# First output projection: products ordered by high and low weights, transposed tiles ahead of weights, last two tiles normalised one by one

## The chip, the core and the metric

The kernel runs on one core of a Trainium2 chip. The metric is the device time of one execution in microseconds (us), here the median of three runs. The five instruction queues of the core are PE (TensorE, with PEld for its loads of the stationary operand), DVE (VectorE), ACT (ScalarE), POOL (GpSimd) and SP (SyncE, which issues the transfers here). Each takes its instructions in the order in which the program wrote them, and they wait for each other through semaphores.

## The reference, cut to what matters

The program computes three blocks one after the other on 1024 tokens of width 1024. The stage in question is the end of the first block and the layer norm that opens the second:

```python
y = jnp.concatenate([y_conv, y_ret], axis=-1) @ w_out[l]     # (1024, 2048) @ (2048, 1024)
h = h + gate * y
return _rmsnorm(h, final_g)
...
x = layer_norm(x, ln_in_g, ln_in_b)                          # second block, LN_EPS = 1e-5
proj = x @ w_in + b_in                                       # what follows the stage
```

## The kernel before

**Splitting.** Every float32 matrix product is made of three products of reduced parts. A tile is split into a high part (ScalarE copies it to the type fp32r) and a low part (VectorE subtracts the high part from the original), and PE adds up hi*hi, hi*lo and lo*hi in the same PSUM bank (`products`, L370 to L372). The low*low product is left out in both kernels.

**Tiling.** The projection contracts 2048 channels in NK = 16 steps of 128 (`K_ORDER`: the eight tiles of the retention half `yr`, then the eight of the convolution half `yc`). Its eight token tiles of 128 go in three groups, `O_GROUPS` = (0,1,2), (3,4,5), (6,7), because each token tile of a group needs a pair of PSUM banks (2 x 512 columns) for the whole group: `bank_of` = pair 0, pair 3, pair 2. A step of group 0 or 1 is 3 tokens x 2 halves x 3 products = 18 matmuls of 128x128 on 128x512, a step of group 2 is 12. In all 16 x 18 + 16 x 18 + 16 x 12 = 768.

**Weights.** Each step needs one tile of `w_out` (128x1024): SP loads it into `wo_raw` (two buffers, L1306, after the low part two tiles before it is made), ACT makes `wo_hi` (L1422, after PE has finished the step two before, semaphore `wo_used`), DVE makes `wo_lo` (L1293, after `wo_hi`). In group 0 the same loops also split the input tile into `yr_hi`/`yc_hi` (L1424) and `yr_lo`/`yc_lo` (L1298). The last two tiles of a group serve the first two steps of the next, so 44 tiles are loaded for 48 steps. PE waits at the head of a step for `wo_lo` (semaphore `o1_wlo`).

**End of a group.** When a token tile's sums are complete (`o1_mm`), DVE multiplies them by the gate into `tmp` (L1474, which frees the bank pair: `gate_ok`, in the rows below `o1_gate`), and adds the residual tile `xo` (L1476). ACT squares and takes the root (L1450, L1455), DVE scales and takes the statistics (L1479 to L1485), ACT takes the second root (L1460), DVE centres and finishes (L1489, L1494), and `h_ok` (in the rows `o1_h`) is raised. SP stores the tile as `h`. In the next group, ahead of its steps 10, 11 and 12, PE transposes the three tiles (L1358), ACT makes `h_hi` of the transposed tile (L1431) and DVE `h_lo` (L1500). `highs(upto)` and `out_lows(upto)` are the places in the queues of ACT and DVE at which the parts of the next weights are made.

**Behind the last group** PE computes the first half (512 tokens) of the channels 0, 1 and 2 of the next projection (`channel`, 24 matmuls each), transposes tiles 6 and 7, and computes the second halves, channel 0 by the loop at L1400 to L1404. The channel weights are split by ACT (`ch_hi`, L1648) and POOL (`ch_lo`, L1690). ACT's `ch_hi` of channel 0 stands behind the last `h_hi` of group 1's tiles and waits until tile 5 is stored (`h2_out[2]`), since it reuses that buffer.

## Time and profile before

| | |
|---|---|
| median of 3 runs | 2764.65 us (2763.58 to 2766.03) |
| span of the profiled execution | 2763.9 us |
| PE busy | 2689.4 us, 97% |
| DVE busy | 2086.6 us, 75% |
| ACT busy | 1069.2 us, 39% |
| POOL busy | 477.0 us, 17% |
| share of the chain that ended last | PE 80%, DVE 14%, issue 2%, ACT 1%, DMA 1% |

The profile is of one execution, and the trace gives its span from the first to the last instruction. The page counts how long each engine was busy. The timeline lists the instructions of an engine by their start, with the idle time before one in brackets and what released it. A matmul's printed duration (0.39 us) is longer than the distance to the next one, since matmuls overlap; distances are taken between starts. The chain of waits follows the end of the program back from releaser to releaser.

### The profile page before, as it was taken

The page shows a single profiled execution, that of the slowest core. Times are in us where ns is not written, and L with a number is a line of the kernel's source. Part 1 is how long each engine was busy: PE and PEld are TensorE (multiplying, and loading weights), DVE is VectorE, ACT ScalarE, POOL GpSimd, SP SyncE. Part 2 cuts the span into 40 slices and gives each one's busy share as a digit, 9 for nine tenths or more (in the row PEclk, how much of TensorE's full clock was granted, in tenths as well). Part 3 has the DMA queues.
Part 4 walks back from the last instruction along what each step waited for, and adds up shares of the span by engine and source line. Part 5 has one row for each costly group of instructions (what it writes and reads, how often), then busy time and mean ns, then how long its engine had stood idle before and what let it go on. Part 6 is the DMA issues. An engine that isn't in the chain of part 4 may idle for free.

```text
span 2763.9 us, 33573 instructions
## 1 busy us (share of the span) xinstructions
PE 2689.4 (97%) x13192; PEld 2199.6 (80%) x13192; DVE 2086.6 (75%) x2796; ACT 1069.2 (39%) x1599; POOL 477.0 (17%) x254
## 2 busy tenths in 40 slices
PE   6999999999999999999999999999999999999998
PEld 5888888888888878778875678888887888888887
DVE  6999998873724663369998886688186988887978
ACT  5111112243413332245537751365232554555332
POOL 0000000000100002001210001354211656655000
PEclk8999999999999999999999999999999999999999
DMA  5312222224325452011101032100132222225431
GB/s 223 116 63 69 94 97 61 84 92 142 99 107 175 136 176 90 31 62 39 47 30 36 32 123 96 46 31 23 62 115 80 96 77 89 87 77 188 170 99 61
DMA packets 97710, 250.18 MB, mean 91 GB/s; under 512 B 7361, under 2 KB 34369, under 8 KB 96018
## 3 DMA queue, kind: packets, MB, share of 16 engines
q1 hardware_dynamic: 93010, 231.49, 24.4%
q10 hardware_dynamic: 4288, 15.73, 1.5%
q8 instruction: 105, 1.72, 0.2%
q0 software_dynamic: 256, 0.82, 0.1%
q14 instruction: 51, 0.42, 0.1%
HBM read 202.92 MB, written 45.09 MB: 90 GB/s over the span
## 4 chain that ended last, share of the span: by engine, by line
PE 80%; DVE 14%; issue 2%; ACT 1%; DMA 1%; DVEq 0%; ACTq 0%
PE pair L370 16%; PE pair L372 16%; PE pair L371 16%; PE pair L3657 7%; PE pair L3242 5%; PE pair L3244 5%; PE pair L3245 5%; DVE counted L1942 3%; PE pair L2593 2%; DVE reached L1993 1%; PE pair L2156 1%; DVE top_i L1999 1%; PE pair L1754 1%; PE pair L2172 1%; PE pair L2185 1%
## 5 line engine op out<-in xcount | busy, mean ns | idle before, releaser
L370 PE MATMUL pair<-u_hi,w_hi 128*128 128x512 f32 x768 | 302.1, 393 | 1.2 <-PEq L92 0.9
L641 DVE SCALAR_TENSOR_TENSOR conv_acc<-aT,cols,conv_acc 128x1024 f32<-128x1024 f32 x232 | 297.9, 1284 | 6.7
L371 PE MATMUL pair<-u_lo,w_hi 128*128 128x512 f32 x768 | 300.3, 391 | 0.0
L372 PE MATMUL pair<-u_hi,w_lo 128*128 128x512 f32 x768 | 300.3, 391 | 0.0
L370 PEld LDWEIGHTS pair<-u_hi,w_hi 128*128 128x128 f32 x768 | 145.2, 189 | 32.7 <-issue 2.4
L371 PEld LDWEIGHTS pair<-u_lo,w_hi 128*128 128x128 f32 x768 | 145.0, 189 | 30.6 <-issue 0.7
L372 PEld LDWEIGHTS pair<-u_hi,w_lo 128*128 128x128 f32 x768 | 145.0, 189 | 30.6
L370 PE MATMUL pair<-h_hi,ch_hi 128*128 128x512 f32 x392 | 153.8, 392 | 2.8 <-ACT ch L1824 2.6
L372 PE MATMUL pair<-h_hi,ch_lo 128*128 128x512 f32 x392 | 152.7, 389 | 0.0
L371 PE MATMUL pair<-h_lo,ch_hi 128*128 128x512 f32 x392 | 152.6, 389 | 0.0
L1014 POOL TENSOR_TENSOR yrT<-yrT,gate_c 128x1024 f32<-128x1024 f32 x8 | 18.9, 2366 | 758.1 <-ACT yrT L907 758.1
L3192 POOL TENSOR_TENSOR op_lo<-w_sum,op_hi 128x512 fp32r<-128x512 f32 x80 | 137.6, 1721 | 33.6 <-ACT op_hi L3322 33.6
L454 DVE TENSOR_TENSOR w_lo<-wt,w_hi 128x1024 fp32r<-128x1024 f32 (+1 forms) x64 | 69.8, 1091 | 77.0 <-ACT w_hi L450 76.9
L3242 PE MATMUL pair<-t_hi,op_hi 128*128 128x512 f32 x320 | 124.6, 389 | 0.0
L3245 PE MATMUL pair<-t_hi,op_lo 128*128 128x512 f32 x320 | 124.5, 389 | 0.0
L3244 PE MATMUL pair<-t_lo,op_hi 128*128 128x512 f32 x320 | 124.5, 389 | 0.0
L1690 POOL TENSOR_TENSOR ch_lo<-wt,ch_hi 128x1024 fp32r<-128x1024 f32 x17 | 40.7, 2395 | 464.7 <-ACT ch_hi L1648 464.7
L450 ACT ACTIVATE w_hi<-wt 128x1024 fp32r<-128x1024 f32 (+1 forms) x64 | 60.8, 950 | 142.8 <-PE pair L372 135.3
L1293 DVE TENSOR_TENSOR wo_lo<-wo_raw,wo_hi 128x1024 fp32r<-128x1024 f32 x44 | 54.0, 1228 | 66.5 <-ACT wo_hi L1422 66.4
L370 PE MATMUL pair<-h_hi,p_hi 128*128 128x512 f32 x256 | 103.6, 405 | 0.0
L372 PE MATMUL pair<-h_hi,p_lo 128*128 128x512 f32 x256 | 100.2, 392 | 0.0
L371 PE MATMUL pair<-h_lo,p_hi 128*128 128x512 f32 x256 | 99.7, 389 | 0.0
(510 smaller groups left out, 7105.1 us busy)
## 6 DMA issues: line engine op xcount, KB each, us to landing
wt<-in_w_ch SPq DMA_DIRECT2D x60, 512.0 KB, 3.4
wo_raw<-in_w_out SPq DMA_DIRECT2D x44, 512.0 KB, 3.6
wt<-in_w_up SPq DMA_DIRECT2D x10, 1024.0 KB, 4.9
w_raw<-in_w_up SPq DMA_DIRECT2D x10, 1024.0 KB, 4.8
g_spill<-g_stage SPq DMA_DIRECT2D x40, 256.0 KB, 2.2
ada_mod<-in_ada_mod SPq DMA_DIRECT2D x4, 2048.0 KB, 14.3
wt<-in_w_conv SPq DMA_DIRECT2D x16, 512.0 KB, 3.5
qk<-qk_st SPq DMA_DIRECT2D x8, 1024.0 KB, 6.4
```

The source lines that it names most:

```text
L370: nc.tensor.matmul(bank, w[0], x[0], start=(first and k == 0), stop=False)
L371: nc.tensor.matmul(bank, w[0], x[1], start=False, stop=False)
L372: return nc.tensor.matmul(bank, w[1], x[0], start=False, stop=(last and k == n_k - 1))
L450: nc.scalar.activation(slot_view(w_parts[0], n), slot_view(wt, n), ACT.Copy).then_inc(job_hi, 1)
L454: nc.vector.tensor_tensor(slot_view(w_parts[1], n), slot_view(wt, n), slot_view(w_parts[0], n).bitcast(F32), ALU.subtract).then_inc(job_lo, 1)
L641: nc.vector.scalar_tensor_tensor(dst, x, w, conv_acc[:], ALU.mult, ALU.add).then_inc(conv_step, 1)
L1942: nc.vector.tensor_scalar(to, scores(t), least, None, op, ALU.add, accum_out=found[:, t - 2:t - 1]).then_inc(counts_ok, 1)
L3192: nc.gpsimd.tensor_tensor(op_lo[j], operand(w, j), op_hi[j].bitcast(F32), ALU.subtract).then_inc(op_lo_ok, 1)
L3242: nc.tensor.matmul(bank, hi[:, k, :], x_hi[:, k, :], start=(j in opens and k == 0), stop=False, skip_group_check=True)
L3244: nc.tensor.matmul(bank, hi[:, k, :], x_lo[:, k, :], start=False, stop=False, skip_group_check=True)
L3245: last = nc.tensor.matmul(bank, lo[:, k, :], x_hi[:, k, :], start=False, stop=(k == 3), skip_group_check=True)
L3657: last = nc.tensor.matmul(dn_bank(p, t), x[:, i, t * P:(t + 1) * P], w[:, i, :], start=(p in (P1, P7, P2) and c == kind == i == 0), stop=( ...
```

## The change

It edits only this stage. On PE a step no longer runs through `products` token by token: all tokens' hi*hi come first, then all x_lo*w_hi, then all x_hi*w_lo, and the waits for `x_hi`, `x_lo`, `wo_hi` and `wo_lo` stand each ahead of the products that use the part. On ACT and DVE `h_hi` and `h_lo` of a transposed tile come one weight tile earlier in the queue (`at0 + 11 + j` for `at0 + 12 + j`). For the last group, roots and reciprocals are made for each tile by itself, tile 6 is finished before tile 7 is centred, and the transposes of tiles 6 and 7 stand inside the first half of channel 2.

```diff
--- before.py
+++ after.py
@@ -1365,35 +1365,46 @@
                 k = K_ORDER[s % NK]
                 if g and i in (10, 11, 12):
                     transposes(3 * (g - 1) + i - 10)
-                pe.wait_ge(wo_lo_ok, s + 1)
+                pe.wait_ge(wo_hi_ok, s + 1)
                 if g == 0:
-                    pe.wait_ge(x_lo_ok, i + 1)
-                for j, t in enumerate(O_GROUPS[g]):
-                    if g and i == 0:
-                        pe.wait_ge(gate_ok, 3 * (g - 1) + j + 1)
-                    if n == 0 and j == 0:
-                        pe.wait_ge(ot_ok, KT * TT)
-                    if n == 0 and j == 1:
-                        pe.wait_ge(pw_out, KT - 1)
-                    for h in range(2):
-                        last = products(bank_of[j][:, h, :],
-                                        [x[:, k % KT, t * P:(t + 1) * P] for x in x_parts(k)],
-                                        [w[:, s % 2, h * HALF:(h + 1) * HALF] for w in wo_parts], i, NK)
-                    if i == NK - 1:
-                        last.then_inc(o1_mm, 1)
+                    pe.wait_ge(x_hi_ok, i + 1)
+                x_hi, x_lo = x_parts(k)
+                w_hi, w_lo = (w[:, s % 2, :] for w in wo_parts)
+                for x, w in ((x_hi, w_hi), (x_lo, w_hi), (x_hi, w_lo)):
+                    if x is x_lo and g == 0:
+                        pe.wait_ge(x_lo_ok, i + 1)
+                    if w is w_lo:
+                        pe.wait_ge(wo_lo_ok, s + 1)
+                    for j, t in enumerate(O_GROUPS[g]):
+                        if x is x_hi and w is w_hi:
+                            if g and i == 0:
+                                pe.wait_ge(gate_ok, 3 * (g - 1) + j + 1)
+                            if n == 0 and j == 0:
+                                pe.wait_ge(ot_ok, KT * TT)
+                            if n == 0 and j == 1:
+                                pe.wait_ge(pw_out, KT - 1)
+                        for h in range(2):
+                            last = nc.tensor.matmul(bank_of[j][:, h, :], x[:, k % KT, t * P:(t + 1) * P],
+                                                    w[:, h * HALF:(h + 1) * HALF],
+                                                    start=(i == 0 and x is x_hi and w is w_hi),
+                                                    stop=(i == NK - 1 and w is w_lo))
+                        if i == NK - 1 and w is w_lo:
+                            last.then_inc(o1_mm, 1)
                 if i == NK - 1:
                     pe.wait_ge(o1_mm, O_GROUPS[g][-1] + 1)
                     pe.sem_inc(wo_used, 1)
                 else:
                     last.then_inc(wo_used, 1)
-            for n in range(3):
-                if n == 1:
-                    pe.wait_ge(gate_ok, 7)
-                if n == 2:
-                    pe.wait_ge(gate_ok, 8)
-                channel(pe, n, 0)
-            for t in O_GROUPS[-1]:
-                transposes(t)
+            channel(pe, 0, 0)
+            pe.wait_ge(gate_ok, 7)
+            channel(pe, 1, 0)
+            pe.wait_ge(gate_ok, 8)
+            for k in range(KT):
+                if k == KT - 3:
+                    transposes(TT - 2)
+                if k == KT - 2:
+                    transposes(TT - 1)
+                channel_step(pe, 2, k)
             pe.wait_ge(tr_ok, TT)
             bank, w_hi, w_lo = pair[CH_PAIR[0]][:, 1, :], ch_hi_of(0), ch_part_lo[0]
             for k in range(KT):
@@ -1449,17 +1460,25 @@
                         act.wait_ge(sq_done, t)
                     nc.scalar.activation(junk1[:], xo[j][:], ACT.Square,
                                          accum_out=ssq[:, j:j + 1]).then_inc(sq_done, 1)
+                    if g == 2:
+                        act.wait_ge(sq_done, t + 1)
+                        nc.scalar.activation(sd1[:, j:j + 1], ssq[:, j:j + 1], ACT.Sqrt, bias=eps6[:],
+                                             scale=1.0 / D).then_inc(rms_ok, 1)
                     if j == 1:
                         highs(at0 + 3)
-                act.wait_ge(sq_done, tokens[-1] + 1)
-                nc.scalar.activation(sd1, ssq, ACT.Sqrt, bias=eps6[:], scale=1.0 / D).then_inc(rms_ok, 1)
-                highs(at0 + 6)
                 if g == 2:
                     channel_high(act, 2)
-                act.wait_ge(bnv_ok, tokens[-1] + 1)
-                nc.scalar.activation(sd2, mv1[:, :, 1], ACT.Sqrt, bias=eps5[:]).then_inc(sd_ok, 1)
+                    for j, t in enumerate(tokens):
+                        act.wait_ge(bnv_ok, t + 1)
+                        nc.scalar.activation(sd2[:, j:j + 1], mv1[:, j, 1:2], ACT.Sqrt, bias=eps5[:]).then_inc(sd_ok, 1)
+                else:
+                    act.wait_ge(sq_done, tokens[-1] + 1)
+                    nc.scalar.activation(sd1, ssq, ACT.Sqrt, bias=eps6[:], scale=1.0 / D).then_inc(rms_ok, 1)
+                    highs(at0 + 6)
+                    act.wait_ge(bnv_ok, tokens[-1] + 1)
+                    nc.scalar.activation(sd2, mv1[:, :, 1], ACT.Sqrt, bias=eps5[:]).then_inc(sd_ok, 1)
                 for j, t in enumerate(tokens):
-                    highs(at0 + 12 + j)
+                    highs(at0 + 11 + j)
                     evacuate(t)
                 if g == 1:
                     act.wait_ge(h2_out[2], 32)
@@ -1516,7 +1535,7 @@
                 at0 = NEW * (g + 1)
                 if g:
                     for j, t in enumerate(O_GROUPS[g - 1]):
-                        out_lows(dve, NEW * g + 12 + j)
+                        out_lows(dve, NEW * g + 11 + j)
                         low_part(t)
                 out_lows(dve, at0 + 2)
                 add(0, tokens[0])
@@ -1524,6 +1543,19 @@
                 for j, t in enumerate(tokens[1:]):
                     add(j + 1, t)
                 out_lows(dve, at0 + 3)
+                if g == 2:
+                    for j, t in enumerate(tokens):
+                        dve.wait_ge(rms_ok, 3 + j)
+                        nc.vector.reciprocal(rr1[:, j:j + 1], sd1[:, j:j + 1]).then_inc(rr_ok, 1)
+                        dve.wait_ge(rr_ok, 3 + j)
+                        normalize(j, t)
+                    for j, t in enumerate(tokens):
+                        center(j, t)
+                        dve.wait_ge(sd_ok, 3 + j)
+                        nc.vector.reciprocal(rv1[:, j:j + 1], sd2[:, j:j + 1]).then_inc(rv_ok, 1)
+                        dve.wait_ge(rv_ok, 3 + j)
+                        finish(j, t)
+                    continue
                 dve.wait_ge(rms_ok, g + 1)
                 nc.vector.reciprocal(rr1, sd1).then_inc(rr_ok, 1)
                 dve.wait_ge(rr_ok, g + 1)
```

PE, group 0 to group 1. Before, the next group's first step takes token 0 with six matmuls and then waits for token 1's pair (`pair<-` names the matmul's output, behind it the moving and the stationary operand):

```order
L371 MATMUL pair<-wo_lo,yc_hi 128x512
L372 MATMUL pair<-wo_hi,yc_lo 128x512
L370 MATMUL pair<-wo_hi,yc_hi 128x512 [waits o1_mm,o1_gate,o1_wlo]
L371 MATMUL pair<-wo_lo,yc_hi 128x512
L372 MATMUL pair<-wo_hi,yc_lo 128x512
L370 MATMUL pair<-wo_hi,yc_hi 128x512
L371 MATMUL pair<-wo_lo,yc_hi 128x512
L372 MATMUL pair<-wo_hi,yc_lo 128x512
L370 MATMUL pair<-wo_hi,yc_hi 128x512 [waits o1_gate]
```

PE, the same place after; the first two rows are the end of group 0's last step:

```order
L1387 MATMUL pair<-wo_lo,yc_hi 128x512 [waits o1_wlo]
L1387 MATMUL pair<-wo_lo,yc_hi 128x512 x5
L1387 MATMUL pair<-wo_hi,yc_hi 128x512 [waits o1_mm,o1_gate,o1_whi]
L1387 MATMUL pair<-wo_hi,yc_hi 128x512
L1387 MATMUL pair<-wo_hi,yc_hi 128x512 [waits o1_gate]
L1387 MATMUL pair<-wo_hi,yc_hi 128x512
L1387 MATMUL pair<-wo_hi,yc_hi 128x512 [waits o1_gate]
L1387 MATMUL pair<-wo_hi,yc_hi 128x512
L1387 MATMUL pair<-wo_hi,yc_lo 128x512 x6
L1387 MATMUL pair<-wo_lo,yc_hi 128x512 [waits o1_wlo]
L1387 MATMUL pair<-wo_lo,yc_hi 128x512 x5
```

The waits for the three bank pairs now stand two matmuls apart instead of six, and the low parts' products stand last.

ACT, the end of group 1's tiles, before:

```order
L1422 ACTIVATE wo_hi<-wo_raw 128x1024 [waits o1_used,wo_in0]
L1431 ACTIVATE h_hi<-pair 128x8x128 [waits o1_tr]
L1422 ACTIVATE wo_hi<-wo_raw 128x1024 [waits o1_used,wo_in1]
L1431 ACTIVATE h_hi<-pair 128x8x128 [waits o1_tr]
L1648 ACTIVATE ch_hi_677<-wt 128x1024 [waits ch_w0,h2_out2]
L1422 ACTIVATE wo_hi<-wo_raw 128x1024 [waits o1_used,wo_in0]
L1422 ACTIVATE wo_hi<-wo_raw 128x1024 [waits o1_used,wo_in1]
L1648 ACTIVATE ch_hi_678<-wt 128x1024 [waits ch_w1,o1_mm]
```

and after:

```order
L1433 ACTIVATE wo_hi<-wo_raw 128x1024 [waits o1_used,wo_in0]
L1442 ACTIVATE h_hi<-pair 128x8x128 [waits o1_tr]
L1680 ACTIVATE ch_hi_677<-wt 128x1024 [waits ch_w0,h2_out2]
L1433 ACTIVATE wo_hi<-wo_raw 128x1024 [waits o1_used,wo_in1]
L1433 ACTIVATE wo_hi<-wo_raw 128x1024 [waits o1_used,wo_in0]
L1433 ACTIVATE wo_hi<-wo_raw 128x1024 [waits o1_used,wo_in1]
L1680 ACTIVATE ch_hi_678<-wt 128x1024 [waits ch_w1,o1_mm]
```

Three weight tiles' high parts, those of steps 41 to 43 of the 44 loaded (counted from 0), stand behind `ch_hi_677` and its wait for the store `h2_out2`, where two did before.

PE, the last two tiles, after:

```order
L1358 MATMUL pair<-ident,xo_611 128x128 [waits h2_lo_ok,o1_h]
L1358 MATMUL pair<-ident,xo_611 128x128 x7
L370 MATMUL pair<-h_hi,ch_hi_679 128x512
L371 MATMUL pair<-h_lo,ch_hi_679 128x512
L372 MATMUL pair<-h_hi,ch_lo_676 128x512
L1358 MATMUL pair<-ident,xo_612 128x128 [waits o1_h]
L1358 MATMUL pair<-ident,xo_612 128x128 x7
```

Before, both sets of transposes stood behind the whole of channel 2's first half; now nine of its matmuls follow the first set, three of them ahead of the second.

## Rows read from the trace of the kernel before

**Rows 1.** The page: span, and granted clock in 40 slices.
```profile
span 2763.9 us, 33573 instructions
...
PEclk8999999999999999999999999999999999999999
```

**Rows 2.** Windows by stretch; busy us and count of each engine, then clock.
```profile
914.00:983.00 69.00, 68.15 (x312) 56.05 (x311) 43.09 (x43) 21.50 (x25) 0.00 (x0) 1.00 0.51 152
983.00:1042.00 59.00, 52.17 (x229) 39.69 (x227) 44.48 (x45) 22.37 (x26) 2.41 (x1) 1.00 0.50 152
1042.00:1067.00 25.00, 23.64 (x111) 19.43 (x111) 21.14 (x31) 9.73 (x12) 5.18 (x2) 1.00 0.41 144
```

**Rows 3.** Chain that ended last, 980 to 1043: by line; start, us, what.
```profile
by line: DMA wo_raw<-in_w_out 23.7%; DVE wo_lo L1293 17.2%; DVE small L1483 6.2%; DVE xo L1479 5.9%; DVE xo L1476 5.9%; DVE tmp L1474 5.9%; PE pair L370 5.5%; ACT wo_hi L1422 5.1%; PE pair L372 5.1%; PE pair L371 5.1%; DVE xo L1494 3.9%; DV
...
1013.87 3.62 DMA wo_raw<-in_w_out
1019.86 6.00 DMA wo_raw<-in_w_out
```

**Rows 4.** Waits of PE, 836 to 1095: total us, times, longest.
```profile
PE pair L370 <- DVE wo_lo L1293: 4.8, 7, 1.5
PE pair L1358 <- DVE h_lo L1500: 1.6, 2, 1.2
```

**Rows 5.** Timeline of PE: start, us, instruction [idle before <-releaser].
```profile
867.17 0.47 PE L370 MATMUL pair<-wo_hi,yr_hi 128*128 128x512 f32 x1 [0.74 <-DVE yr_lo L1298]
...
913.51 0.39 PE L370 MATMUL pair<-wo_hi,yc_hi 128*128 128x512 f32 x1
...
916.00 0.39 PE L372 MATMUL pair<-wo_hi,yc_lo 128*128 128x512 f32 x1
916.70 0.47 PE L370 MATMUL pair<-wo_hi,yc_hi 128*128 128x512 f32 x1 [0.30 <-PE pair L372]
...
920.23 0.50 PE L370 MATMUL pair<-wo_hi,yc_hi 128*128 128x512 f32 x1 [0.55 <-DVE tmp L1474]
```

**Rows 6.** Timeline of DVE: yr_lo, two multiplies, and the slow add.
```profile
865.80 1.22 DVE L1298 TENSOR_TENSOR yr_lo<-yrT,yr_hi 128x1024 fp32r<-128x1024 f32 x1
...
913.71 1.23 DVE L1474 TENSOR_TENSOR tmp<-pair,gate_bc 128x1024 f32<-128x1024 f32 x1 [1.93 <-PE pair L372]
...
918.95 1.23 DVE L1474 TENSOR_TENSOR tmp<-pair,gate_bc 128x1024 f32<-128x1024 f32 x1
...
1044.57 2.11 DVE L1476 TENSOR_TENSOR xo<-xo,tmp 128x1024 f32<-128x1024 f32 x1
```

**Rows 7.** Timeline of ACT at the end of group 2.
```profile
1029.74 1.06 ACT L1422 ACTIVATE wo_hi<-wo_raw 128x1024 fp32r<-128x1024 f32 x1 [1.88 <-DMA wo_raw<-in_w_out]
...
1031.61 1.05 ACT L1648 ACTIVATE ch_hi<-wt 128x1024 fp32r<-128x1024 f32 x1
```

**Rows 8.** Timeline of SP's queue; landing of stores, 1010 to 1062.
```profile
1024.35 0.43 SPq L1313 DMA_DIRECT2D h<-xo  x1
...
DMA to landing us min/median/max: 2.6/5.2/6.9
```

**Rows 9.** Timeline of PE at the last two tiles.
```profile
1058.58 2.16 PE L1358 MATMUL pair<-ident,xo 128*128 128x128 f32 x16
...
1061.91 0.50 PE L1400 MATMUL pair<-h_hi,ch_hi 128*128 128x512 f32 x1 [1.17 <-ACT h_hi L1435]
1062.25 0.40 PE L1401 MATMUL pair<-h_hi,ch_lo 128*128 128x512 f32 x1
...
1065.71 0.62 PE L1404 MATMUL pair<-h_lo,ch_hi 128*128 128x512 f32 x2
```

**Rows 10.** Timeline of DVE and POOL at the last two tiles.
```profile
1040.69 1.23 DVE L1474 TENSOR_TENSOR tmp<-pair,gate_bc 128x1024 f32<-128x1024 f32 x1 [2.26 <-PE pair L372]
...
1048.23 0.18 DVE L1528 RECIPROCAL small<-small 128x3 f32<-128x3 f32 x1 [1.55 <-ACT small L1455]
...
1043.19 2.41 POOL L1690 TENSOR_TENSOR ch_lo<-wt,ch_hi 128x1024 fp32r<-128x1024 f32 x1 [8.05 <-ACT ch_hi L1648]
```

## The prediction

> **What bounds the kernel now.** I read the page first. Its span and its clock row [rows 1] say that TensorE (PE) is busy nearly always at the full granted clock, so what can be won is the little that PE stands idle in the edited stage, and what can be lost is any new idle time there. The stage is the first output projection, from about 850 to 1067 us of the span. The windows by stretch [rows 2] give the size of the prize. In group 1 (914 to 983) PE is idle 0.85 of 69 us, in group 2 (983 to 1042) 6.83 of 59, in the tail (1042 to 1067) 1.36 of 25. With 0.74 at 867 the stage holds some 10 us of idle PE, 0.4% of the time. Then I asked what sets the length of each stretch. Group 1 is PE's own: 18 matmuls a step, one every 0.2265 us (from 913.51 to 916.00 there are 11 [rows 5]), 4.08 us a step. Group 2 is not: the chain that ended last [rows 3] holds PE for only 16% there; its largest parts are the weight transfers (23.7%), VectorE's low parts (17.2%) and VectorE's adds and normalisation. After the stage, PE or the work released by it is the chain, without any earlier start that could absorb a shift, so I carry a shift of the stage's end to the end one for one.
>
> The profiled execution has a span of 2763.9 us; the median of the three runs is 2764.65, 0.75 above it. I work out a difference against the trace and add it to the median. This kernel's measurement can tell about 0.2% (5.5 us) from no change, so faster means under 2759.1, slower over 2770.2.
>
> **Part 1, PE starts a step with the high parts.** Once in group 0 and seven times in group 2, PE stands before a step's first matmul until VectorE's low parts are there [rows 4, 5]. In group 0 this is the step at 867.17 [rows 5]: it waited for yr_lo, made from 865.80 to 867.02 [rows 6]; its high parts had been ready at 865.6. The last matmul before it began at 866.04, so in the new order the step begins at 866.27 and wants yr_lo for its matmuls 7 to 12, at 867.6. The hole goes: 867.17 - 866.27 and 0.1 of refill, **-1.0**. The rest of group 0 is PE's own pace, so it is kept.
>
> **Part 2, what the same reordering does to the end of a group.** This is the cost, and it follows from the order. Before, a step finishes token 0's bank pair after 6 of its 18 matmuls, token 1's after 12, token 2's after 18, and the next group begins with six matmuls on token 0. After, all hi*hi come first, then lo*hi, then hi*lo, so the three bank pairs of the last step finish after 14, 16 and 18 matmuls, and in the next group's first step PE wants token 1's pair after two matmuls and token 2's after four (the waits for o1_gate in the order above). VectorE frees each pair with one multiply, and its queue has multiply, add, multiply, add, multiply: the multiplies start at 913.71, 916.33 and 918.95, 2.62 us apart [rows 6] (the second has no row there), so the pairs come free 1.23 us after each.
> First place, group 0 to group 1: the first multiply can start 8 matmuls later, 8 x 0.2265 = 1.81 us, so 915.52; pairs free at 916.75, 919.37, 921.99. PE, at the old times, starts on token 0 at 916.8 (before 916.70), on token 1 at 919.4 and on token 2 at 922.0, and has 14 matmuls left, 14 x 0.2265 + 0.1 refill = 3.3: the step ends at 925.3. Before, token 2 began at 920.23 with 6 matmuls left: 920.23 + 1.36 + 0.1 = 921.7 [rows 5]. **+3.6**. Nothing hides it: ScalarE's next high part waits for that step's end, and group 1 is at PE's pace throughout.
> The Trainium skill (Perfetto Trace Analysis, section Matmuls) says that independent groups of matmuls should rotate through PSUM banks so that the evacuation of one overlaps the next one's matmuls. It speaks against this change. Read strictly, with nothing left to overlap, the multiply would start only with the 18th matmul, 4 x 0.2265 = 0.9 later, and this term would be 4.5; the issue order still leaves that 0.9, so the sum keeps 3.6.
> Second place, group 1 to group 2: two tokens only. PE's first step would end 2.3 us later (pair 1 free at 987.56 + 1.23 = 988.8, 10 matmuls left, 991.2, against 988.9). But here PE is not what counts. From 983.1, the group's first multiply, to 1013.9 the chain runs through VectorE's queue, where the low parts lie between adds and normalisations; from there on the weight loop sets the pace (low part, transfer of 3.6 to 6.0, high part 1.07, low part 1.23) [rows 3]. All of it starts with the first multiply, so it moves by **+1.8**. Against this stands the only place where part 1 pays in group 2: PE needs the low part for a step's last 4 matmuls of 12, not the first, so a step ends 4 matmuls after its low part and no longer 12: 8 x 0.2265 = **-1.8**. The two cancel. The sum of the waits that the trace shows in group 2 is so no gain: it is the slack of an engine that waits for a supply whose length the change doesn't shorten.
>
> **Part 3, transposes served ahead of weights.** Twice in group 2 (1.6 us in all [rows 4]) PE waits for h_lo of the previous tile before it transposes the next, because VectorE's h_lo stands behind a low part whose weights have not landed. With the new order these two waits go, but PE then only reaches the next weights sooner. Worked through with the trace's durations (times below include the +1.8): transposes at 1020.6, 1024.3 and 1027.9, step 40 ends at 1031.5 instead of 1033.0, and step 41 finds no high part: its weights land at 1031.5, since their transfer is released by low part 39. Gain nil. In the new order of ScalarE's queue, moreover, the high part of step 41 has gone behind ch_hi, which waits until the last of the first six tiles is stored. Before, the queue had high part 41 at 1029.74, h_hi, then ch_hi at 1031.61 without a wait [rows 7]. The store is issued behind the weights' transfer, at 1024.35, and stores here land in 5.2 us (median) to 6.9 (longest) [rows 8]; with 1.8 added, 1031.4 to 1033.1. High part 41 then starts at 1032.4 to 1034.1 instead of 1031.5, and so do low part 41, transfer 43, high part 43 and the last step. It would end at 1042.3 to 1043.9, against 1041.85: +0.5 to +2.1, I take **+1.3**, the middle, since the transfers around it are at the long end (6.0 and 5.3 us). If the store is early, it is 0. In group 1 the same move costs nothing: a step of 4.08 us covers h_hi and h_lo, and the next high part is needed only at its end.
>
> **Part 4, the last two tiles one by one.** Before: PE has finished channel step 2 at about 1058.5, transposes at 1058.58 and 1059.81, and goes on at 1061.91 [rows 9]. After, the transposes stand before the sixth and seventh k of that channel, 15 matmuls in, at 1056.5 at the earliest. VectorE decides. Its first multiply comes 4 matmuls later, 1040.69 + 0.91 = 1041.60. Two multiplies and adds take 5.99 us with the slow add of 2.11 beside POOL [rows 6, 10]: 1047.6. ScalarE's root for tile 6 is long done, so the idle 1.55 us before 1048.23 goes. Then reciprocal 0.21, normalisation 2.77, reciprocal 0.21, normalisation 3.35 with its slow instruction, centre 1.22, reciprocal 0.21, finish 1.22: tile 6 ready at 1056.8; centre, reciprocal, finish 2.7 more: tile 7 at 1059.5, against 1059.6 before. If the two slow instructions (0.88 and 0.58 over the ordinary 1.23 and 1.28) miss POOL, they are 1055.3 and 1058.0. From the second transposes to L1400 it took 2.10 us [rows 9]; with 6 matmuls behind the transposes 2.25. PE goes on between 1060.5 and 1061.9: -1.5 to 0. I take **-0.8**. The extra small instructions (ScalarE two roots more of 0.30, VectorE two reciprocals more of 0.2) are in these sums. The third channel's low part is wanted at 1053.1 and was made by 1052.0; it comes at most 0.9 later.
> The Trainium skill (GPSIMD Engine Reference, section Key points) says that GpSimd shares its SBUF interfaces with VectorE and contends with instructions with two SBUF inputs. The rows agree: the add of xo and tmp took 2.11 us beside ch_lo, the multiply out of PSUM 1.23. By that rule both adds would now meet ch_lo, this term would be about 0, and the sum 0.8 higher; the rows at hand show one slow add at a time, so the middle stands.
>
> **Sum.** -1.0 + 3.6 + (1.8 - 1.8) + 1.3 - 0.8 = **+3.1 us**: 2764.65 + 3.1 = **2767.7**. Bounds: low -1.0 + 3.4 - 0.5 + 0 - 1.5 = +0.4, high -0.9 + 3.8 + 0.5 + 2.1 - 0 = +5.5 (0.2 on the gate for latencies, 0.5 on the cancelling pair), so the likeliest case has 2765.0 to 2770.2.
>
> **Rivals.**
> A, the low parts really were the brake. If VectorE and the transfers can run ahead in group 2 once PE no longer waits for the low part, all 6.8 us of idle time there [rows 2] go and only PE's own stall of 2.3 comes: -1.0 + 3.6 - 6.8 + 2.3 - 0.8 = -2.7, 2762.0. For it: the waits view names wo_lo as the longest. Against: the chain [rows 3]. If the gate stall at the first place were missing too, it would be -6.3, 2758.3, faster; against that stands VectorE's strict sequence of 2.62 us.
> B, slower: matmuls come less densely. The new order changes the bank with every matmul where the old one did so every third, and the stationary tile every second. The old rows show no gap at a change of bank. But where L1400 and L1401 alternate, 15 matmuls take 3.46 us, 0.2307 each, from 1062.25 to 1065.71 [rows 9]. The stage has 768 matmuls: 768 x (0.2307 - 0.2265) = 3.2 us more, 2770.9. It decides from 0.230 on: then 2.5 us more carry the time over 2770.2.
>
> **How the numbers follow.** The forecast 66%, A 14% (about half of it below 2759.1, with the stall missing or other gains), B 20%, with what of a worse tail goes beyond 2.1. The range: cutting a tenth at either side gives 2761.5 to 2772.0. Faster 0.08, same 0.72, slower 0.20: of the forecast hardly anything lies over 2770.2, of B nearly all.
>
> **What would show it.** Right: in the first step of group 1 two stops of about 2.2 us each before L1387, released by the multiply into tmp; no wait at 867; the first step of group 1 some 3.6 us longer; in group 2 PE's waits now mostly for wo_hi, with the stretch as long as before or 1 to 2 us longer; ch_hi waiting for a store ahead of high part 41; the pause around the last transposes smaller by about 1 us. Wrong: group 2 shorter by several us (A), or matmuls spaced over 0.230 us inside a step (B).

## The result, and the profile after

The changed kernel takes **2774.95 us** (median of 6 runs, 2773.9 to 2776.56), the kernel before 2764.69 (6 runs). The ratio is 1.0038, with a 95% interval of 1.0026 to 1.0049. The forecast was 2767.7 with a range up to 2772.0: the direction of the sum was right, its size was not, and the time is outside the range. The kernel became slower by more than the 0.2% that can be told.

To see where, I cut the edited stage at five matmuls that both traces have (start times in the timelines of TensorE): the first matmul of the first output projection, the first of group 1, of group 2, of the channel work, and the first of channel 0's second half (L1400 before, L1411 after).

| stretch, us | before | after | difference | forecast |
|---|---|---|---|---|
| group 0 | 66.78 | 65.97 | -0.81 | -1.0 |
| group 1 | 69.42 | 74.76 | +5.34 | +3.6 |
| group 2 | 56.04 | 58.63 | +2.59 | +1.3 |
| tail | 19.75 | 20.36 | +0.61 | -0.8 |
| together | 211.99 | 219.72 | +7.73 | +3.1 |

Outside these stretches the span grew by another 1.4 us (0.46 ahead of the stage, 0.92 behind it). Nothing there is edited, and the traces of all twelve kernels put the start of the stage anywhere from 848.6 to 850.4 and the rest behind it at 1701.5 to 1704.0, so I don't count it as the change's.

The page has a longer span and the same clock row as before [rows 1]:

```profile
span 2773.1 us, 33578 instructions
...
PEclk8999999999999999999999999999999999999999
```

Finer windows tell what those 40 digits can't. They answer to [rows 2] (columns: TensorE busy and count, weight loads, VectorE, ScalarE, GpSimd, granted clock, DMA share, GB/s):

```profile
914.00:918.00 4.00, 2.55 (x11) 1.49 (x9) 2.85 (x3) 0.50 (x1) 0.00 (x0) 1.00 0.00 0
918.00:922.00 4.00, 1.72 (x3) 1.00 (x4) 3.80 (x4) 1.80 (x4) 0.00 (x0) 0.54 0.00 0
922.00:926.00 4.00, 4.00 (x12) 3.09 (x11) 0.70 (x1) 0.00 (x0) 0.00 (x0) 0.61 0.00 0
926.00:930.00 4.00, 4.00 (x19) 3.27 (x19) 1.96 (x3) 2.40 (x4) 0.00 (x0) 1.00 0.00 0
930.00:985.00 55.00, 55.00 (x256) 45.77 (x255) 34.06 (x35) 16.80 (x17) 0.00 (x0) 1.00 0.57 182
985.00:992.00 7.00, 6.30 (x27) 4.62 (x25) 2.23 (x2) 0.00 (x0) 0.00 (x0) 1.00 0.25 75
992.00:998.00 6.00, 4.37 (x13) 3.48 (x14) 5.12 (x5) 2.52 (x5) 0.00 (x0) 0.72 0.02 4
```

From 918 to 926 TensorE is granted 0.54 and 0.61 of its clock, so for most of the time the lower of its two levels, 1.2 GHz. Windows cut still finer put the whole fall between 918.3 and 925.2:

```profile
917.10:918.30 1.20, 0.00 (x0) 0.00 (x0) 1.07 (x2) 0.80 (x1) 0.00 (x0) 1.00 0.00 0
918.40:925.10 6.70, 4.82 (x11) 3.34 (x12) 4.10 (x4) 1.40 (x4) 0.00 (x0) 0.50 0.00 0
```

The window from 922 to 926 is fully busy and holds 12 matmuls instead of 19. The same happens at 992 to 998, at the edge of groups 1 and 2. The rest of group 1 (930 to 985) is without a hole and at full clock. TensorE's timeline at the first edge, beside [rows 5] (start, us, instruction, idle before and its releaser):

```profile
914.33 1.52 PE L1387 MATMUL pair<-wo_lo,yc_hi 128*128 128x512 f32 x6
916.35 0.70 PE L1387 MATMUL pair<-wo_hi,yc_hi 128*128 128x512 f32 x2 [0.50 <-DVE tmp L1493]
918.88 1.22 PE L1387 MATMUL pair<-wo_hi,yc_hi 128*128 128x512 f32 x2 [1.82 <-DVE tmp L1493]
921.50 1.22 PE L1387 MATMUL pair<-wo_hi,yc_hi 128*128 128x512 f32 x2 [1.40 <-DVE tmp L1493]
922.52 2.76 PE L1387 MATMUL pair<-wo_hi,yc_lo 128*128 128x512 f32 x6
925.08 1.59 PE L1387 MATMUL pair<-wo_lo,yc_hi 128*128 128x512 f32 x6
926.51 1.54 PE L1387 MATMUL pair<-wo_hi,yc_hi 128*128 128x512 f32 x6
927.89 1.52 PE L1387 MATMUL pair<-wo_hi,yc_lo 128*128 128x512 f32 x6
```

The two stops that the forecast named are here, 1.82 and 1.40 us, each ended by VectorE's multiply. What it did not have is the row at 922.52: six matmuls in 2.56 us (to 925.08), where six take 1.36 at 927.89 (to 929.25). The 14 matmuls from 921.50 to 926.51 needed 5.0 us instead of 3.3. The clock was already low at 918.4, inside the first stop (917.06 to 918.88) and ahead of the second.

Group 2 loses its first time in a place that the forecast had called unimportant. VectorE's timeline after, and the same low part (tile 30) before:

```profile
989.73 1.22 DVE L1493 TENSOR_TENSOR tmp<-pair,gate_bc 128x1024 f32<-128x1024 f32 x1 [4.88 <-PE pair L1387]
...
998.87 1.23 DVE L1293 TENSOR_TENSOR wo_lo<-wo_raw,wo_hi 128x1024 fp32r<-128x1024 f32 x1 [1.42 <-ACT wo_hi L1433]
```

```profile
990.77 1.22 DVE L1293 TENSOR_TENSOR wo_lo<-wo_raw,wo_hi 128x1024 fp32r<-128x1024 f32 x1
```

Counted from group 2's first matmul (986.12 before, 991.11 after), this low part starts at 4.65 before and at 7.76 after. ScalarE's high part ahead of it is the reason, since it may overwrite its buffer only when TensorE has ended the slowed first step. Then, at the end of the group, comes the store wait that the forecast did have, beside [rows 7]:

```profile
997.78 1.06 ACT L1433 ACTIVATE wo_hi<-wo_raw 128x1024 fp32r<-128x1024 f32 x1 [1.76 <-PE pair L1387]
...
1037.47 1.06 ACT L1680 ACTIVATE ch_hi<-wt 128x1024 fp32r<-128x1024 f32 x1 [1.50 <-DMA h<-xo]
1038.43 1.04 ACT L1433 ACTIVATE wo_hi<-wo_raw 128x1024 fp32r<-128x1024 f32 x1
```

The store wait had company that the forecast did not have. Behind channel 0's high part GpSimd makes its low part, and in the new queue order that falls on VectorE's low part of tile 41, which takes 2.56 us where the low part of tile 30 above took 1.23. (Before, it met the low part of tile 42, which took 1.60.) It ends 1.08 us behind GpSimd; what that means is worked out under e8.

```profile
1038.60 2.38 POOL L1722 TENSOR_TENSOR ch_lo<-wt,ch_hi 128x1024 fp32r<-128x1024 f32 x1 [260.67 <-ACT ch_hi L1680]
...
1039.50 2.56 DVE L1293 TENSOR_TENSOR wo_lo<-wo_raw,wo_hi 128x1024 fp32r<-128x1024 f32 x1 [2.27 <-ACT wo_hi L1433]
```

The chain that ended last, by line, from 990 to 1043, answers to [rows 3]: TensorE's products now hold 29.0% of it and the weight transfers 12.4%, against 16% and 23.7%.

```profile
by line: PE pair L1387 29.0%; DVE wo_lo L1293 15.5%; DMA wo_raw<-in_w_out 12.4%; DVE small L1502 7.3%; DVE xo L1498 7.0%; issue 6.2%; PE pair L1358 4.9%; DVE tmp L1493 4.7%; DVE xo L1508 4.6%; ACT wo_hi L1433 4.1%; DVE xo L1513 2.4%; DVE xo
```

In the tail the idle 1.55 us of [rows 10] is gone, but tile 7's normalisation takes 2.99 us beside GpSimd's low part, where tile 6's takes 1.28; the transposes wait for it twice:

```profile
1055.12 1.28 DVE L1498 SCALAR_TENSOR_TENSOR xo<-xo,small,fg_bc 128x1024 f32<-128x1024 f32 x1
...
1058.04 2.99 DVE L1498 SCALAR_TENSOR_TENSOR xo<-xo,small,fg_bc 128x1024 f32<-128x1024 f32 x1
...
1057.56 2.39 POOL L1722 TENSOR_TENSOR ch_lo<-ch_raw,ch_hi 128x1024 fp32r<-128x1024 f32 x1 [3.63 <-ACT ch_hi L1680]
...
1065.19 1.09 PE L1358 MATMUL pair<-ident,xo 128*128 128x128 f32 x8 [0.92 <-DVE xo L1513]
...
1067.78 1.09 PE L1358 MATMUL pair<-ident,xo 128*128 128x128 f32 x8 [0.80 <-DVE xo L1513]
```

### The profile page after: what moved, and what is told of

Read it like the earlier page. It is cut to its first block, busy times and chain, and to the rows that moved or that the text cites. A ratio compares the mean times of both kernels' runs of the same rounds, so it can differ in the third digit from the quotient of the medians.

```text
span 2773.1 us, 33578 instructions
## 1 busy us (share of the span) xinstructions
PE 2694.8 (97%) x13192; PEld 2202.8 (79%) x13192; DVE 2083.1 (75%) x2798; ACT 1070.4 (39%) x1601; POOL 479.5 (17%) x254
## 4 chain that ended last, share of the span: by engine, by line
PE 83%; DVE 11%; issue 2%; ACT 1%; DMA 0%; DVEq 0%; ACTq 0%
PE pair L370 15%; PE pair L372 15%; PE pair L371 15%; PE pair L3689 7%; PE pair L1387 5%; PE pair L3276 5%; PE pair L3274 5%; PE pair L3277 5%; DVE counted L1974 2%; PE pair L2625 2%; DVE reached L2025 1%; PE pair L2188 1%; PE pair L1786 1%; PE pair L2204 1%; PE pair L2217 1%
```

## The experiments

Two questions stood: what of the loss is the edge between groups, and why the clock falls; and what of the loss at the end of group 2 and in the tail is the order of ScalarE's queue. All edits are to the changed kernel, unless said otherwise. The stage lengths of all, in us (cut as above), beside the ratio to the kernel before on the same chip:

| kernel | group 0 | group 1 | group 2 | tail | together | ratio [95%] |
|---|---|---|---|---|---|---|
| before | 66.78 | 69.42 | 56.04 | 19.75 | 211.99 | |
| after | 65.97 | 74.76 | 58.63 | 20.36 | 219.72 | 1.0038 [1.0026, 1.0049] |
| e1 | 65.77 | 69.41 | 59.68 | 19.60 | 214.46 | 1.0007 [0.9998, 1.0015] |
| e2 | 65.97 | 71.21 | 58.54 | 20.36 | 216.08 | one run |
| e3 | 65.97 | 73.01 | 59.10 | 20.36 | 218.44 | 1.0030 [1.0018, 1.0043] |
| e4 | 65.97 | 74.77 | 59.25 | 20.49 | 220.48 | 1.0029 [1.0017, 1.0041] |
| e5 | 65.97 | 74.50 | 57.50 | 20.36 | 218.33 | 1.0023 [1.0014, 1.0033] |
| e6 | 65.77 | 69.40 | 54.34 | 20.35 | 209.86 | 0.9992 [0.9983, 1.0001] |
| e7 | 65.77 | 69.40 | 53.23 | 20.36 | 208.76 | 0.9991 [0.9982, 0.9999] |
| e8 | 65.97 | 75.31 | 59.49 | 20.49 | 221.26 | 1.0031 [1.0019, 1.0043] |
| e9 | 65.77 | 69.40 | 54.10 | 19.45 | 208.72 | 0.9987 [0.9978, 0.9996] |
| e10 | 65.97 | 74.70 | 60.30 | 19.46 | 220.43 | 1.0029 [1.0018, 1.0041] |

Groups 0 and 1 and the tail repeat within some 0.3 us wherever their code is the same; e8's group 1, 0.55 over that of after, is the exception. Group 2 doesn't: e10 has exactly the code of after there and took 1.67 us more. Of this, 1.50 is there when ScalarE starts channel 0's high part (47.86 us behind the group's first matmul, 46.36 in after), which had waited 2.75 us for the store instead of 1.50. So much of the scatter is that store wait, which is part of the change's own cost and differs from run to run. A single trace can tell differences of 2 us or more in group 2; smaller ones are indications.

**e1, products token by token in each group's last step and in the first step of groups 1 and 2.**

```diff
+                if (g and i == 0) or i == NK - 1:
+                    pe.wait_ge(wo_lo_ok, s + 1)
...
+                    for j, t in enumerate(O_GROUPS[g]):
...
+                            last = products(bank_of[j][:, h, :],
...
+                else:
                     for x, w in ((x_hi, w_hi), (x_lo, w_hi), (x_hi, w_lo)):
```

> The changed kernel, but in the last step of each group and in the first step of the next the products run token by token again, as before the change; all other steps start with the high parts. Theory S (the loss is made at the group edges: the three bank pairs come free late, PE stops twice, and its granted clock falls to half): no stops in the first step of group 1 beyond the old 0.3 and 0.55 us, clock 1.00 there; group 1 begins its second step near 921.0 and not 926.5; group 2 still gets its low parts at VectorE's pace, but starts its adds 1.8 us earlier than the changed kernel and ends each step 4 matmuls after the low part, so the first channel matmul comes near 1041 to 1042 and not at 1049.7. Total 2766 to 2768 us, of which 1.3 to 2.5 are the ch_hi behind the store and the tail. Rival R (the reordering costs everywhere, by a wider spacing of matmuls or by later release of the weights): still over 2771 us, with the surplus spread over all steps.

Measured: 2767.64 us. Group 1 is back at 69.41, the whole 5.35 us. So the entire loss of group 1 is made in the steps at the edges, and the new order costs nothing in the 14 others. Group 2 gained nothing, at 59.68. Channel 0's high part waited 2.15 us for the store, and TensorE stood for 2.52 us ahead of the step of tile 41. Then the group's own last step, now wanting its low part first, waited 1.94 us and ran at the lower clock:

```profile
1030.40 1.20 PE L1401 MATMUL pair<-wo_hi,yc_hi 128*128 128x512 f32 x4 [2.52 <-ACT wo_hi L1447]
...
1038.86 0.50 PE L370 MATMUL pair<-wo_hi,yc_hi 128*128 128x512 f32 x1 [1.94 <-DVE wo_lo L1293]
1039.17 0.62 PE L371 MATMUL pair<-wo_lo,yc_hi 128*128 128x512 f32 x1
1039.59 0.63 PE L372 MATMUL pair<-wo_hi,yc_lo 128*128 128x512 f32 x1
```

The last two start 0.42 us apart, not 0.2265. Behind the longer pause of 2.52 us the clock stayed at 1.00 (windows from 1028 to 1038.8). The expectation had the first channel matmul at 1041 to 1042; it came at 1043.59.

**e2, only the first steps of groups 1 and 2 token by token.** The edit is that of e1 with the condition `g and i == 0`.

> The changed kernel, but only the first step of groups 1 and 2 runs token by token; in the last step of each group the bank pairs are still finished after 14, 16 and 18 matmuls. VectorE's multiplies then start 1.8 us later than in e1, 2.62 us apart, and PE reaches token 1 after six matmuls and token 2 after twelve. Theory S: token 1's pair is free 2.6 us after PE's start on token 0, 1.4 needed, so a stop of about 1.2 us, then another of 1.2; the first step of group 1 ends near 923.5 in the changed kernel's times (926.5), about 2.5 us after e1. Whether the clock falls for stops of 1.2 us is open: if it doesn't, the clock belongs to the length of the stops and not to their number. Rival R: no difference to e1.

Measured: 2769.58 us in its one run, group 1 at 71.21, 1.79 over before. The stops at the edge are shorter, with six matmuls between them instead of two:

```profile
918.72 0.50 PE L370 MATMUL pair<-wo_hi,yc_hi 128*128 128x512 f32 x1 [0.90 <-DVE tmp L1507]
...
921.33 0.50 PE L370 MATMUL pair<-wo_hi,yc_hi 128*128 128x512 f32 x1 [0.96 <-DVE tmp L1507]
921.67 0.39 PE L371 MATMUL pair<-wo_lo,yc_hi 128*128 128x512 f32 x1
```

From the second one behind each stop on the matmuls are 0.23 us apart: no fall of the clock. What is left, 1.79, is near the 8 x 0.2265 = 1.81 by which the last step in the new order frees its first bank pair later. The stops were shorter than the 1.2 us expected.

**e3, the stops filled.** Ahead of the waits for the second and third pair, TensorE first waits for the idle pair `pair[1]` to be free and does 8 matmuls into it, whose result nobody reads. It does the same work as the changed kernel otherwise, and those 16 or 8 matmuls more at each edge.

```diff
                             if g and i == 0:
+                                if j:
+                                    pe.wait_ge(pw_out, KT)
+                                    if g == 2:
+                                        pe.wait_ge(h2_lo_ok, 3)
+                                    for _ in range(8):
+                                        nc.tensor.matmul(pair[1][:, 0, :], x[:, k % KT, t * P:(t + 1) * P],
+                                                         w[:, 0:HALF], start=True, stop=True)
                                 pe.wait_ge(gate_ok, 3 * (g - 1) + j + 1)
```

> The changed kernel, with eight idle matmuls (into a free bank, results unused) ahead of each wait for a further bank pair in the first steps of groups 1 and 2, which last 1.8 us and lie inside the stops of 1.8 and 1.4 us plus a margin. The waits for VectorE stay as they are. Theory S with the clock as a part of its own: PE never pauses for over 0.5 us, the granted clock stays at 1.00, the first step of group 1 ends 1.7 us earlier (near 924.8), and group 2 gets its first high part about 1 us earlier; total 2 to 3 us below the changed kernel, 2772 to 2773. If the clock has no part in it, the total is the same as the changed kernel's or more, 2775 and above.

Measured: 2774.0 us, group 1 at 73.01. The same windows as above, in e3:

```profile
918.00:922.00 4.00, 3.97 (x17) 2.74 (x16) 3.80 (x4) 1.19 (x3) 0.00 (x0) 1.00 0.00 0
922.00:926.00 4.00, 4.00 (x20) 3.30 (x19) 0.56 (x2) 1.57 (x2) 0.00 (x0) 1.00 0.00 0
...
992.00:998.00 6.00, 6.00 (x28) 4.91 (x27) 5.42 (x6) 4.72 (x7) 0.00 (x0) 1.00 0.13 18
```

The clock stays at 1.00, and the first matmuls on the three bank pairs start at 915.74, 918.27 and 920.89, as far apart as in after (2.53 and 2.62 us), so this splits the loss of group 1: 73.01 - 69.42 = 3.59 us is the late bank pairs, which is what the forecast had (3.6), and 74.76 - 73.01 = 1.75 is the lower clock. (The other traces with this edge, e4, e5, e8 and e10, lie between 74.50 and 75.31, so the clock's part is 1.5 to 2.3.) In group 2, too, the low part of tile 30 starts 6.30 us behind the first matmul (995.05 and 988.75 in the timelines) instead of 7.76: 1.65 of the delay was the late multiply (forecast 1.8), 1.46 the clock. As a whole e3 gained 1.3 us in the stage by the trace. Its ratio is 0.0008 lower, 2.2 us, well inside the two intervals, which reach some 3 us to either side. The expectation of no pause over 0.5 us failed later in group 2, where TensorE paused 3.11 us ahead of the step of tile 41, behind a store wait of 2.74.

**e4, the reordering alone.** Parts 3 and 4 undone (`at0 + 12 + j`, and the tail of the kernel before).

> Only the reordering of the products: h_hi and h_lo of transposed tiles again behind one more weight tile, last two tiles normalised together and transposed behind channel 2, as before the change. Theory S: both stops and the clock's fall are there as in the changed kernel (second step of group 1 at 926.5), the channels start near 1048.5 instead of 1049.7, since high part 41 is not held up by the store, and the tail costs 0.5 us less: total 2772 to 2774. If the two other parts were gains that the reordering hides, it would be above the changed kernel's 2775.

Measured: 2773.83 us, group 2 at 59.25, tail 20.49. The waits for h_lo, which the forecast had disappear with part 3, are here; one of them is 2.30 us long, and behind it the clock falls again (the four matmuls from 1034.89 start 0.43 us apart; TensorE's timeline):

```profile
1032.69 1.06 PE L1358 MATMUL pair<-ident,xo 128*128 128x128 f32 x8 [2.30 <-DVE h_lo L1509]
1033.51 1.58 PE L1387 MATMUL pair<-wo_hi,yr_hi 128*128 128x512 f32 x4
1034.89 1.91 PE L1387 MATMUL pair<-wo_hi,yr_lo 128*128 128x512 f32 x4
```

The stage as a whole is as long as after's (220.48 and 219.72): the reordering alone makes the loss, and parts 3 and 4 as written give nearly nothing back. Two expectations failed here: the channels were to start near 1048.5 and did at 1050.0, and the tail was to cost 0.5 less than after's and cost 0.13 more.

**e5, channel 0's high part behind tile 41's.**

```diff
                 if g == 1:
+                    highs(at0 + 14)
                     act.wait_ge(h2_out[2], 32)
                     channel_high(act, 0)
```

> The changed kernel; the only edit is that ScalarE makes the high part of weight tile 41 ahead of ch_hi and its wait for the store of tile 5, as it stood before the change. Theory Q (that wait held up tile 41 and with it transfer 43 and the last two steps): high part 41 about 1.5 to 2 us earlier, PE's pause before it (1.88 us) gone, first channel matmul 1.5 to 2.5 us earlier than the changed kernel's when both are taken from the group's first matmul (58.6 us there), so 56.1 to 57.1; total 1.5 to 2.5 us under the changed kernel. Rival (the transfers of the last tiles, slow beside stores and residual loads, set the end of the group whatever ScalarE does): the pause moves to the next tile and the stretch keeps 58 us or more.

Measured: 2772.06 us, group 2 at 57.50, 1.13 less than after and 1.75 less than e4. The wait for the store is still there, but no weight stands behind it:

```profile
1035.12 1.06 ACT L1433 ACTIVATE wo_hi<-wo_raw 128x1024 fp32r<-128x1024 f32 x1 [0.90 <-DMA wo_raw<-in_w_out]
1036.38 1.06 ACT L1681 ACTIVATE ch_hi<-wt 128x1024 fp32r<-128x1024 f32 x1 [0.20 <-DMA h<-xo]
```

The low part of tile 41 now takes 1.23 us, since GpSimd's subtraction (1037.52, 2.39 us) meets no low part. So the edit takes away two costs at once, and the 1.13 doesn't split them. The rival was right in part: TensorE's pause ahead of tile 41 shrank from 1.88 to 0.33 us, but one of 1.35 stands ahead of tile 42, and the stretch is longer than the 56.1 to 57.1 expected. Against e4, serving transposes first looks worth something in itself, but e4 also has the lower clock behind its pause of 2.30. Both differences are inside the scatter of group 2, and no run settles this one.

**e6, edges and channel 0's high part together.** As e1, but the last step of group 2 keeps the new order (`(g and i == 0) or (i == NK - 1 and g < 2)`), with the line of e5.

> Both costs taken out: products token by token in the last steps of groups 0 and 1 and in the first steps of groups 1 and 2, all others (the last step of group 2 too) with the high parts first, and ch_hi behind the high part of tile 41. Theory S + Q: no pause of PE over 1 us in groups 1 and 2, clock 1.00 throughout, group 1 begins its second step about 5 us earlier than the changed kernel, group 2 lasts 54 to 55.5 us from its first matmul to the first channel matmul (56.0 in the kernel before), total 2 to 3 us under the kernel before, ratio 0.999. Rival (group 2 is bound by the supply of weights however PE orders its products): group 2 lasts 56 us or more, total within 1 us of the kernel before.

Measured: 2763.4 us, ratio 0.9992. Group 2 is at 54.34: 4.3 under after, 3.16 under e5, and 1.70 under before. Low part 30 starts 4.65 us behind the first matmul, as before. The 3.16 between e5 and e6 is what the edge costs in group 2, and agrees with how much later low part 30 starts (2.98 in e5, 3.11 in after). The 1.70 under before is mostly the gain that the forecast put at 8 x 0.2265 = 1.8: from the end of the group's last low part to the first channel matmul it is 3.73 us before and 2.26 here, 1.47 less, while that low part itself ends only 0.24 earlier. e7 and e9, also with normal edges and no weight behind the store, have 53.23 and 54.09, below the 56.05 of before as well. One pause of 1.27 us was left, where the expectation had none over 1.

**e7, the loads of the last two residual tiles behind the last weight's.** As e6; on SyncE the residual loads and store waits of the last three transposed tiles move behind the loop over weights.

```diff
-                if g and i in (13, 14, 15):
+                if g == 1 and i in (13, 14, 15):
...
+            for t in (3, 4, 5):
+                sp.wait_ge(h2_out[t % 3], 16 * (t // 3 + 1))
+                sp.wait_ge(tr_mm, t + 1)
+                if t + 3 < TT:
+                    residual(t + 3)
```

> As the run with both costs taken out, and the residual loads of tiles 6 and 7, with the waits for stores ahead of them, are issued behind the last weights' transfer instead of between the last three. If the slow transfers of tiles 40 to 42 (5.3 to 6.0 us against 3.6) come from these loads and stores beside them, tile 42 lands 1 to 2 us earlier and group 2 is 0.5 to 1.5 us shorter. If they come from the stores alone, which are issued two tiles earlier, nothing changes. Should a residual tile land after VectorE wants it, its add waits and the tail grows.

Measured: 2763.0 us, group 2 at 53.23. That is 1.1 less than e6, inside the scatter of this group, and e9 with the same code there had 54.10; the ratios are 0.9991 and 0.9992. I count it as not settled.

**e8, the tail of the kernel before.** Only part 4 undone.

> The changed kernel with its last part undone: tiles 6 and 7 normalised together, transposed behind the first half of channel 2. The tail from the first channel matmul to the first matmul of channel 0's second half took 20.36 us in the changed kernel, 19.75 in the kernel before, and 20.49 in the reordering alone. Theory: with PE's last step finishing tile 6 two matmuls from its end instead of six, the old tail costs 20.4 to 20.6 here, so part 4 is worth 0.1 to 0.2 us and the total doesn't move; its gain was eaten by the later start of VectorE's chain (0.9 us) and by one normalising instruction of 2.99 us beside POOL. Rival (part 4 itself costs): the tail falls to 19.8 us or less.

Measured: 2774.16 us, tail 20.49 against 20.36. In the changed kernel part 4 is worth 0.13 us. The tail is 0.61 over that of before in after and 0.74 in e4 and e8, because the new order of the last step hands over its first bank pair 4 matmuls (0.9 us) later; with that step token by token (e1) it is 19.60.

Why only 0.13? The traces have one regularity. After: GpSimd's low part ends at 1057.56 + 2.39 = 1059.95, the long normalisation at 1058.04 + 2.99 = 1061.03, 1.08 later. The slow add of after (1053.06, 1.96 us) ends 1.09 behind GpSimd's 1050.77 + 3.16. In the traces of before, e1 and e8 it is 1.08 to 1.10 again, whatever the duration (1.86, 1.87, 2.11, 2.69, 2.99). The slow instruction is one that waits until GpSimd has ended and then does its work: 1.08 is a little less than its ordinary 1.23 or 1.28, and the spans on GpSimd are rough. The low part of tile 41 in after is such a case too (1038.60 + 2.38 = 1040.98, and 1039.50 + 2.56 = 1042.06). The Trainium skill says this (SBUF — State Buffer, section SBUF: two separate sides): VectorE operations with two SBUF inputs and GpSimd's hold a shared pair of ports as an exclusive lock, and the other one blocks fully. The constant distance of these rows agrees with it. The next two runs test it.

**e9, GpSimd's low part of channel 2 started later.** As e7, with one line moved:

```diff
-                    channel_high(act, 2)
                     for j, t in enumerate(tokens):
                         act.wait_ge(bnv_ok, t + 1)
                         nc.scalar.activation(sd2[:, j:j + 1], mv1[:, j, 1:2], ACT.Sqrt, bias=eps5[:]).then_inc(sd_ok, 1)
+                        if j == 0:
+                            channel_high(act, 2)
```

> The kernel of e7 with one line moved on ScalarE: the high part of channel 2 is copied behind the second square root of tile 6, not ahead of it, so that GpSimd's low part of channel 2 starts some 1.4 us later, when tile 7's normalise is (by my reckoning) already over. Theory (GpSimd's subtraction and VectorE's two-input operations on SBUF exclude each other: the later waits until the other ends, then takes its ordinary time; in the changed kernel GpSimd's 1057.56 + 2.39 = 1059.95, and tile 7's normalise of 2.99 us ends 1.08 behind that): tile 7's normalise takes 1.28 us again; its bn_stats, with one input, run through; the centering of tile 6 meets the last of the subtraction and takes about 2.0 us instead of 1.23, ending about 1.1 us behind GpSimd's end. Gain in the tail 1.7 - 0.8 = about 0.9 us: tail 20.36 -> 19.5, time 763.0 -> 762.1 (all plus 2000). Rival (the two slow each other in proportion while they overlap, whichever operation it is): what normalise no longer pays, bn_stats and centering pay between them; the sum stays, tail 20.2 to 20.4, time unchanged.

Measured: tail 19.45. VectorE and GpSimd in e9:

```profile
1047.51 1.28 DVE L1519 SCALAR_TENSOR_TENSOR xo<-xo,small,fg_bc 128x1024 f32<-128x1024 f32 x1
1048.83 1.29 DVE L1523 BATCH_NORM_STATS2 small<-xo 128x6 f32<-128x512 f32 x2
1050.15 0.21 DVE L1525 BATCH_NORM_AGGREGATE small<-small 128x2 f32<-128x12 f32 x1
1050.28 1.99 DVE L1529 SCALAR_TENSOR_TENSOR xo<-xo,small,lg_bc 128x1024 f32<-128x1024 f32 x1
...
1048.81 2.38 POOL L1743 TENSOR_TENSOR ch_lo<-ch_raw,ch_hi 128x1024 fp32r<-128x1024 f32 x1 [5.41 <-ACT ch_hi L1701]
```

The normalisation takes 1.28, the statistics (one input) run through GpSimd's work undisturbed at 1.29, and the centring, caught by its end, stops 1.08 behind it (1052.27 and 1051.19). The rival, a slowdown in proportion, would have shown it in the statistics and left the sum; it falls. The time, 2762.65 us at a ratio of 0.9987, is the best of all kernels here, with an interval that ends below 1, though 0.13% is less than the 0.2% named in the forecast; the step from e7 to e9 is 0.4 us by the medians and 1.1 by the ratios and can't be told from none by the times alone, only by the tail's length.

**e10, the same line moved in the changed kernel.**

> The changed kernel with only that line moved, everything else as in it. Theory: the last part of the change (tiles 6 and 7 normalised one by one) was worth only 0.13 us beside the old tail because GpSimd's subtraction for channel 2 fell on tile 7's normalise; freed of that, tile 7's normalise takes 1.28 us and the tail 20.36 -> 19.5, so that the last part is worth about 1.0 us against the old tail of 20.49, the size that I had predicted (0.8). Time 2774.9 -> 2774.0. Rival: the tail is held by something else (the transposes' place between the matmuls of channel 2), and stays at 20.3 to 20.4 even with a normalise of 1.28 us.

Measured: tail 19.46, normalisation 1.29. Part 4 is now worth 20.49 - 19.46 = 1.03 us. The whole time doesn't show it (2774.06), with a group 2 that took 60.30 in the profiled run.

## Why the prediction was wrong

**Part 1, right.** The wait at 867 is gone; group 0 took 0.81 us less (forecast 1.0).

**Part 2, the first edge: mechanism and price right, a consequence missed.** The late bank pairs cost 3.59 us (e3), forecast 3.6. The step that failed is the sentence "has 14 matmuls left, 14 x 0.2265 + 0.1 refill = 3.3": it took the spacing at full clock for granted behind two stops. They took 5.0 us. Term +3.6, measured +5.34 (or 5.35, e1), of which 1.75 is the clock (e3). At this edge the trace of before gives no warning, since its stops of 0.30 and 0.55 us leave the clock at full. But the forecast wrote of stops of some 2.2 us, and elsewhere in the same trace there is one of 2.11 with the granted clock at 0.57 behind it:

```profile
1158.93 1.35 PE L1754 MATMUL pair<-ch,ch 64*128 64x512 f32 x8 [2.11 <-ACT ch L1821]
...
1160.00:1164.00 4.00, 4.00 (x17) 3.24 (x15) 2.39 (x2) 1.30 (x2) 2.18 (x1) 0.57 0.00 0
```

**Part 2, the second edge.** "But here PE is not what counts" failed. TensorE's first step sets when ScalarE may refill the weight buffers, and with the lower clock that came behind VectorE's own +1.65: low part 30 was 3.11 us late, not 1.8. The other half of the pair, -1.8, was near: e6 has -1.70 once the edge is as before, 1.47 of it by this mechanism. So the pair came to +1.3 where the forecast had 0, with bounds of 0.5.

**Part 3, the size near, in part by luck.** Channel 0's high part waited for the store, ahead of high part 41, as written, and e5 measures 1.13 us (forecast 1.3), within the scatter. But the forecast had only the store in this term. The same queue order also put GpSimd's subtraction on low part 41, which took 1.33 us longer for it (before, low part 42 took 0.37 longer), and e5 takes away both. The store wait alone was 1.50 in after and 2.75 in e10 with the same code. Whether its two waits for h_lo would go without gain stays open: e4 to e5 is -1.75, but with the clock's fall in e4 and within the scatter.

**Part 4, mis-sized.** Forecast -0.8 for the tail, measured +0.61. The 4 matmuls of later start cost 0.74 (e8 against before), forecast 0.9. What failed is "normalisation 3.35 with its slow instruction": I added to tile 7's normalisation the surplus of 0.58 seen before as if it belonged to the instruction. It is a wait until GpSimd ends, and as GpSimd's subtraction and the normalisation now started within 0.5 us of each other, it was 1.7. Of the two adds one waited (1.96 us); the other was there first, took 1.23 and made GpSimd's subtraction longer (3.16). With the subtraction later the tail has -0.29 (e10); the 0.5 between that and the forecast stays open.

**The sum.** Forecast +3.1, stage +7.7. The gap of 4.6 is the clock, 1.75 + 1.46, and the tail, 1.4. The median rose by 10.3, 2.5 more than the stage; the lower end of its interval, 1.0026, is 7.2 us. The other nine kernels' ratios and stage sums agree within 2 us (e6: -2.1 in the stage, -2.2 by the ratio; e5: +6.3 and +6.4).

**Rival A** (low parts are the brake) held only in a weak form: nothing of the 6.8 us went while the edges were late, 1.7 without that (e6), and hardly any of it by an earlier supply (0.24). **Rival B** (matmuls less dense) is false: six matmuls of the new order take 1.36 us, 0.2267 each, as before. The result lay on its side of the forecast, but for another reason. The bounds were too narrow because each was taken at full clock and none allowed for VectorE waiting for GpSimd longer than it had before.

## What to carry to other kernels

When an edit makes TensorE stop between short bursts, allow for what the matmuls behind the stop cost if the granted clock falls, and ask who waits for the end of that burst. An order of products that is better inside a group (all high parts first) can be kept there and the old order used for the steps where banks change hands: that is e6, with a ratio of 0.9992 (up to 1.0001, so not told from the kernel before) where the whole change has 1.0038. When a copy is moved in one engine's queue, look at what the engine behind it will then run beside. And read a slow instruction's end, not its length: if it stands a fixed distance behind another engine's end, it was waiting, and moving that other instruction moves it.
